# A one-core transformer layer in split fp32: six changes around the starts and boundaries of its stages

## The reference

```
h = x
h = h + 0.5 * rmsnorm(swiglu(rmsnorm(h, g_ffn1_pre), gate1, up1, down1), g_ffn1_post)   # width 5632
z = rmsnorm(h, g_mix_pre) @ w_qkv + b_qkv                                              # 4352 columns
oa = dilated_attention(qa, ka, va)      # 16 heads, three patterns merged by their log-sums
ob = sliding_window_gqa(qb, kb, vb, sinks)   # 16 query heads, 2 key heads
o  = concat(rmsnorm(oa, g_out_a), rmsnorm(ob, g_out_b)) @ w_o + b_o
h  = h + rmsnorm(o, g_mix_post)
h  = h + 0.5 * rmsnorm(swiglu(rmsnorm(h, g_ffn2_pre), gate2, up2, down2), g_ffn2_post)
h  = h + rmsnorm(sigmoid(rmsnorm(h, g_ple_pre) @ w_ple_gate) * (p @ w_ple_proj), g_ple_post)
rmsnorm(x, g) = x * rsqrt(mean(x*x) + 1e-6) * g
```

## Time and profile before

| | us |
|---|---|
| median of 3 runs | 1939.09 (1938.91 to 1940.13) |
| the profiled execution: time | 1938.77 |
| the profiled execution: span | 1937.0 |
| PE busy | 1917.0 (99%) |
| DVE busy | 1052.5 (54%) |
| ACT busy | 876.3 (45%) |
| POOL busy | 9.9 (1%) |

### The profile page before, as it was taken

The page is one execution under the profiler, slowest core; times in us unless marked ns, Lnnn a source line. Parts: engine busy times, 40 slices in busy tenths (PEclk is TensorE's granted clock), DMA queues, the critical chain, the costliest instruction groups (busy, mean ns, idle before and its releaser), DMA issues.

```text
span 1937.0 us, 24879 instructions
## 1 busy us (share of the span) xinstructions
PE 1917.0 (99%) x8929; PEld 1589.9 (82%) x8929; DVE 1052.5 (54%) x1227; ACT 876.3 (45%) x1125; POOL 9.9 (1%) x24
## 2 busy tenths in 40 slices
PE   9999999999999999999999999999999999999998
PEld 7888888888888887888888788888888888888886
DVE  5545445444544446766776754545454454444575
ACT  6444444444444345545454544444444443444563
POOL 0000000000000000000000000000000000000000
PEclk9999999999999999999999999999999999999999
DMA  7666666666566654655555566666666665656554
GB/s 241 187 191 188 191 188 187 189 188 191 194 198 197 204 193 142 186 162 154 157 185 168 158 193 186 187 192 189 190 188 191 188 193 197 199 195 205 189 193 142
DMA packets 188483, 361.05 MB, mean 186 GB/s; under 512 B 11440, under 2 KB 16000, under 8 KB 188032
## 3 DMA queue, kind: packets, MB, share of 16 engines
q1 hardware_dynamic: 187408, 356.69, 60.4%
q10 hardware_dynamic: 1008, 3.46, 0.5%
HBM read 358.01 MB, written 2.10 MB: 186 GB/s over the span
## 4 chain that ended last, share of the span: by engine, by line
PE 96%; DVE 1%; DMA 1%; ACT 1%; issue 1%; POOL 0%; ACTq 0%; DVEq 0%; POOLq 0%; SPq 0%
PE bank L451 30%; PE bank L453 30%; PE bank L452 30%; PE bank L550 2%; PE bank L725 1%; PE bank L735 1%; DMA raw<-in_w_qkv 1%; DVE w_rest L1168 0%; PE bank L750 0%; PE bank L749 0%; ACT w_high L865 0%; PE bank L509 0%; PE bank L587 0%; PE bank L748 0%; PE bank L519 0%
## 5 line engine op out<-in xcount | busy, mean ns | idle before, releaser
L1168 DVE TENSOR_TENSOR w_rest<-raw,w_high 128x1024 fp32r<-128x1024 f32 x656 | 802.3, 1225 | 756.5 <-ACT w_high L865 755.4
L865 ACT CAST w_high<-raw 128x1024 fp32r<-128x1024 f32 x656 | 686.9, 1049 | 908.8 <-PE bank L453 900.4
L451 PE MATMUL bank<-w_high,x_high 128*128 128x512 f32 (+1 forms) x1920 | 754.9, 393 | 2.1 <-DVE w_rest L1168 1.8
L453 PE MATMUL bank<-w_high,x_rest 128*128 128x512 f32 (+1 forms) x1920 | 745.6, 388 | 0.0
L452 PE MATMUL bank<-w_rest,x_high 128*128 128x512 f32 (+1 forms) x1920 | 744.3, 388 | 0.0
L451 PEld LDWEIGHTS bank<-w_high,x_high 128*128 128x128 f32 x1920 | 360.8, 188 | 75.9 <-issue 4.6
L453 PEld LDWEIGHTS bank<-w_high,x_rest 128*128 128x128 f32 x1920 | 360.7, 188 | 75.0
L452 PEld LDWEIGHTS bank<-w_rest,x_high 128*128 128x128 f32 x1920 | 361.1, 188 | 70.4
L451 PE MATMUL bank<-w_high,h_high 128*128 128x512 f32 x704 | 274.2, 390 | 0.0
L453 PE MATMUL bank<-w_high,h_rest 128*128 128x512 f32 x704 | 273.9, 389 | 0.0
L452 PE MATMUL bank<-w_rest,h_high 128*128 128x512 f32 x704 | 273.9, 389 | 0.0
(11 more groups left out here) (147 smaller groups left out, 638.0 us busy)
## 6 DMA issues: line engine op xcount, KB each, us to landing
raw<-in_w_ffn_gate SPq DMA_DIRECT2D x176, 512.0 KB, 4.4
raw<-in_w_ffn_up SPq DMA_DIRECT2D x176, 512.0 KB, 3.7
raw<-in_w_ffn_down SPq DMA_DIRECT2D x176, 512.0 KB, 4.3
raw<-in_w_qkv SPq DMA_DIRECT2D x68, 512.0 KB, 3.8
raw<-in_w_o SPq DMA_DIRECT2D x32, 512.0 KB, 3.7
raw<-in_w_ple_gate SPq DMA_DIRECT2D x32, 512.0 KB, 4.5
resid<-in_x SPq DMA_DIRECT2D x8, 256.0 KB, 7.0
gain_row<-in_g_ffn_post SPq DMA_DIRECT2D x8, 256.0 KB, 4.0
```

What stands on the lines that cost most here:

```text
L451: nc.tensor.matmul(o[:, 0:width], xh, wh, start=first and c == 0, stop=False)
L453: ins = nc.tensor.matmul(o[:, 0:width], xr, wh, start=False, stop=last and c == chunks - 1)
L865: nc.scalar.copy(slot(n, k)[0], raw[:, k]).then_inc(w_high_done, 1)
L1168: nc.vector.tensor_tensor(to_rest, raw[:, k], to_high.bitcast(F32), ALU.subtract).then_inc(w_rest_done, 1)
```

## The change

Six edits:

1. The bias row of the first qkv block, whose DMA waits until PE has used all slots before `S_QKV`, is issued by SP behind all 8 loads of the block, and no longer between the fourth and the fifth.
2. `sum_up` is gone from DVE. ACT's squares carry the scale (1/width, times 4 where the branch is halved), and POOL adds the parts one after another (`factor`), each addition waiting for the one before, then takes the power. Where a factor covers both tiles, POOL now works them out one after the other.
3. At both boundaries, the fourth early slot (s=3) is cast and subtracted inside the boundary and no longer ahead of it. DVE does it behind the residual of tile 1.
4. The six small DMAs of FFN1's start are issued one behind each of six later casts.
5. In a lead block that starts at slot 0 (FFN1 and the last gate product), x units are turned in pairs: 2 and 3 behind slot 0, 4 and 5 behind slot 2, 6 and 7 behind slot 4.
6. The first attention-output unit of the second half is turned one slot earlier (`O_TURN_AT`: offset 2 where it was 3).

```diff
-    O_TURN_AT = [NSLOT - KS + 1 + k for k in range(HU)] + [NSLOT + d for d in (3, 4, 7, 12)]
+    O_TURN_AT = [NSLOT - KS + 1 + k for k in range(HU)] + [NSLOT + d for d in (2, 4, 7, 12)]
...
-                load_block(n, w_qkv, RING, col, width=width)
+                before = RING if i else KS
+                load_block(n, w_qkv, before, col, width=width)
                 if i == 0:
                     sp.wait_ge(w_used, S_QKV)
                 sp.dma_start(bias_row[:, col:col + width], b_qkv[:, col:col + width].to_broadcast([P, width])
                              ).then_inc(bias_landed[i % 2], 16)
-                load_block(n, w_qkv, slots, col, s0=RING, width=width)
+                load_block(n, w_qkv, slots, col, s0=before, width=width)
...
+            def factor(job, t):
+
+                n, eps = squares[job] // T, share(job) * EPS
+                part = [stat[:, job, t, b:b + 1] for b in range(n)]
+                pool.wait_ge(squared, Q[job] + T * (n - 2) + t + 1)
+                step(nc.gpsimd.tensor_scalar(msq[:, job, t:t + 1], part[0], eps, None, ALU.add))
+                for b in range(1, n):
+                    if b == n - 1:
+                        pool.wait_ge(squared, Q[job] + T * b + t + 1)
+                    step(nc.gpsimd.tensor_tensor(msq[:, job, t:t + 1], msq[:, job, t:t + 1], part[b], ALU.add))
+                return nc.gpsimd.tensor_tensor(rstd[:, job, t:t + 1], msq[:, job, t:t + 1], minus_half[:, t:t + 1],
+                                               ALU.pow)
...
-                    if s + 2 < KS and s + 2 >= turned_before:
+                    if s0:
+                        if s + 2 < KS:
+                            turn_k(s + 2)
+                    elif s % 2 == 0 and s + 3 < KS:
                         turn_k(s + 2)
+                        turn_k(s + 3)
...
-                high(n0 + RING, 0)
+                high(n0 + RING - 1, RING - 1)
                 x_lead(u0, 0, 1, f, gain)
                 x_lead(u0, 1, 1, f, gain)
+                high(n0 + RING, 0)
                 x_lead(u0, 2, 1, f, gain)
...
-                ahead(n0, KS - 1, KS + 1)
+                for m in range(KS + 1):
+                    ahead(n0, KS - 1 + m, 1)
+                    if between and m < 6:
+                        between(m)
...
-                    ahead(n, S_TURN_P + 1, (FS - 3 if f else FS - 1) - S_TURN_P, k0)
+                    ahead(n, S_TURN_P + 1, (FS - 3 if f else FS - 2) - S_TURN_P, k0)
...
-                sum_up(job, 0, 1)
                 dve.wait_ge(branch_ready, CREDIT + blocks - 1)
                 dve.wait_ge(rstd_ready, factors_up_to(job, 0))
                 for k in range(LEAD):
...
+                rest(n0 + RING - 1, RING - 1)
+                x_rest_lead(u0, 0, 1, f, gain)
                 update(job, LEAD, 0)
-                x_rest_lead(u0, 0, 1, f, gain)
+                x_rest_lead(u0, 1, 1, f, gain)
                 rest(n0 + RING, 0)
-                x_rest_lead(u0, 1, 1, f, gain)
+                x_rest_lead(u0, 2, 1, f, gain)
                 update(job, LEAD + 1, 0)
-                x_rest_lead(u0, 2, 1, f, gain)
                 rest(n0 + RING + 1, 1)
```

More of the change, by code:

```diff
@@ L423, in factors @@
                     done[0] += 1
-                    pool.wait_ge(summed, done[0])
-                    nc.gpsimd.tensor_tensor(rstd[:, job, t0:t1], msq[:, job, t0:t1], minus_half[:, t0:t1], ALU.pow
-                                            ).then_inc(rstd_ready, 1)
-            factors(factors_up_to(J_MIX))
+                    for t in range(t0, t1):
+                        ins = factor(job, t)
+                    ins.then_inc(rstd_ready, 1)
+            factors(factors_up_to(J_POST1))
             pool.wait_ge(w_used, S_QKV)
@@ L1561, in _ @@
                         ins.then_inc(branch_ready, 1)
[L1562 removed]
+                if L < L_END - 1:
+                    rest(S_QKV + L + RING, L % RING)
                 if L == L_KEYS:
```

61 lines of the change are left out of this document (22 added, 39 removed).

## The result

The changed kernel takes 1927.42 us (median of 4 runs, 1927.20 to 1927.57) where the kernel before took 1939.00 (4 runs, 1936.84 to 1940.13): a ratio of 0.9943, 95% interval 0.9931 to 0.9955. The forecast was 1928.3, within 1925.5 to 1931.8. The profiled execution took 1927.20, with a span of 1925.3: 11.7 us less than the span before.

A forecast was written before the change was run, and what follows sets the result against it. PE, busy 99%, bounds the kernel, so only its stops and slow stretches can give time. Terms -2.7 - 6.1 - 1.7 - 0.8 + 0.2 + 0.3 = -10.8 us from 1938.77 gave 1928.0, 1928.3 on the median; range 1925.5 to 1931.8.

The forecast's parts named there:

- FFN1's start: Edits 4 and 5 bring slot 8 from 36.06 to 33.3: -2.7 us, between -1.4 and -3.0.
- POOL's loss of 0.3: Additions on POOL delay its power by 0.1 us: +0.2 entered for both boundaries, +0.1 for the end.
- The DMAs' part: At FFN1's start, casts put ahead of the six small DMAs remove slot 8's 1.5 us delay.
- The pairs' part: At FFN1's start, turning one slot earlier brings unit 7 up to 1.44 us earlier; slots run at 2.7 to 2.83.
- First boundary: Edits 1 to 3: 1.4 us gained before tile 1 is done, 4.7 from there to the fourth slot; together -6.1.
- E: Time when PE has done tile 1 at a boundary and the third unit is turned; 744.96 at the first, before.
- Second boundary: Moving the fourth early rest lets the fourth slot start at 1101.0 against 1102.72: -1.7 us, bounds -0.2 and -2.9.
- the chain of 9.4 us: DVE's work at each boundary from tile 1's residual to the fourth slot's x_rest: updates, x_rests and three rests, 9.4 us.
- The clock held: Rival: the clock falls at the new boundary waits of 1.6 us; one fall gives 1929.8, two 1931.5; chance 0.2.
- half of the terms: Rival: DVE's boundary chain is longer, paired turns stall, half the gain behind tile 1 is lost: 1933; chance 0.07.
- No stall moved on: Rival: PE meets each hindrance one slot later, time within 0.2% of before, 1936 or more; chance 0.03.
- Additions of a microsecond: Sign of being wrong: POOL additions that long, where under 0.54 us was forecast; slow-additions rival, gain gone at 2.6, chance 0.03.

The follow-up runs named there:

- early cast back: Changed kernel with edit 3 undone at both boundaries, so the fourth early slot is cast and subtracted ahead of them: 1931.70 us, ratio 0.9965.
- bias alone: Kernel before with edit 1 alone, the bias DMA behind all eight loads of the first qkv block: 1932.99 us, ratio 0.9969.
- early slot alone: Kernel before with edit 3 alone (fourth early cast and rest moved into the boundary), plus POOL's index patterns moved there: 1931.40 us, ratio 0.9964.
- both back: Changed kernel with edits 1 and 3 both undone: 1936.02 us, ratio 0.9989.
- bias back: Changed kernel with edit 1 undone, the bias DMA again between the fourth and fifth qkv load: 1928.56 us, ratio 0.9949.
- slow sum: Changed kernel with three more dependent additions of a zero on POOL behind the last square of every factor: 1931.39 us, ratio 0.9963.

## Why the prediction was right, point by point

The total came out 0.9 us from the forecast, closer than its parts: FFN1's start gave 0.7 us less than its term, the boundaries 0.5 and 0.8 more, and POOL's loss of 0.3 did not come. That these nearly cancel is luck. The chains that the terms rest on were the right ones, the sharing out among the edits was not.

**What bounds.** Right: four places held all of the gain, PE's standing still there and the clock that fell behind two of the stops, and the table shows the rest of the program unchanged.

**FFN1's start: -2.7 forecast, -2.0 measured.** The DMAs' part is as worked out. The pairs' part was mis-sized: I let all eight slots run at 2.7 to 2.83 us. Timeline of the changed kernel:

```profile
27.25 1.23 DVE L1201 TENSOR_TENSOR w_rest<-raw,w_high 128x1024 fp32r<-128x1024 f32 x1
28.62 0.47 PE L470 MATMUL bank<-w_high,x_high 128*128 128x512 f32 x1
30.17 2.96 ACT L888 CAST w_high<-raw 128x1024 fp32r<-128x1024 f32 x3
31.24 3.50 DVE L1201 TENSOR_TENSOR w_rest<-raw,w_high 128x1024 fp32r<-128x1024 f32 x3 [0.85 <-ACT w_high L888]
31.46 0.39 PE L470 MATMUL bank<-w_high,x_high 128*128 128x512 f32 x1
31.46 3.33 POOL L435 TENSOR_TENSOR msq<-msq,stat 128x1 f32<-128x1 f32 x3
34.18 0.39 PE L470 MATMUL bank<-w_high,x_high 128*128 128x512 f32 x1
```

Slots 6, 7 and 8 start at 28.62, 31.46 and 34.18, in step at last. But slot 7 is only 0.38 us nearer to slot 0 than in the earlier trace rows: slots 2, 4 and 6 still begin when their rests are ready (the rest from 27.25 ends at 28.48, slot 6 starts at 28.62), 0.2 us late each, so an x unit that is ready earlier has nothing to shorten there. The measured term lies within its bounds, but the two edits do not add: either alone gives 1.5.

**First boundary: -6.1 forecast, -6.6 measured.** Ahead of E 1.4 forecast; E stands 3.24 us behind the stretch's start where it stood 4.78, so 1.5. But edit 3, to which the term was booked, is sure of only 0.3 to 0.6 of it. In the two profiles that lack edit 3 but have edit 1, E stands at 3.80 (early cast back) and 3.87 (bias alone), against 3.24 and 3.56 with edit 3 (changed kernel, early slot alone), with a wait of 0.2 to 0.3 us where the kernel before had 1.2. What differs is the landing of the fourth early slot: its cast starts 2.0 us ahead of the stretch there and 1.1 ahead in the kernel before and in both back. The DMAs of the last two down weights, in the 20.5 us that end at the stretch's start (count, KB each, median us from issue to landing), in the kernel before and then with edit 1 alone:

```profile
raw<-in_w_ffn_down SPq DMA_DIRECT2D x2, 512.0 KB, 4.6
```

```profile
raw<-in_w_ffn_down SPq DMA_DIRECT2D x2, 512.0 KB, 3.7
```

These two loads stand ahead of everything that edit 1 touches, so this is scatter between executions and not the edit. Without edit 3 the boundary pays up to 0.9 us of it. With edit 3 it pays nothing: E stands at 3.24 both in the changed kernel, where the four early qkv loads took 4.5 us, and with the bias back, where they took 3.5; this pair also has the late landing with edit 1 and the early one without it. (A late landing may also be part of what the unprofiled runs with the early cast back lost; no trace shows it.) Behind E, 16.2 to 11.5 forecast, 16.2 to 11.1 measured, with a wait of 0.9 and not 1.6 us. The chain I named is the one that ends last. Its size was 0.3 too large, though DVE also stood idle 0.32 us in it for ACT's cast; the reason shows better at the second boundary. What the prediction got wrong in kind is the attribution: it gave all that lies behind E to edit 1. Edit 3 alone does most of it (5.4 us, edit 1 alone 6.8), and given edit 1, edit 3 made this boundary 0.3 longer in the profile, with a load that landed early.

**Second boundary: -1.7 forecast, -2.5 measured** (-2.8 by four other profiles of the same code, 20.8 in the table). Up to an estimated 1.7 us of it is the clock, which the term did not count apart. E was forecast 4.9 us behind the stretch's start (1088.6 less 1083.7) and came 4.9 behind it. Behind E the slot was forecast at +12.4 and came at +11.6. Timeline of the changed kernel:

```profile
1079.29 0.38 PE L506 MATMUL bank<-ident,resid 128*128 128x128 f32 x2
1082.11 1.28 DVE L1225 SCALAR_TENSOR_TENSOR resid<-branch,rstd,resid 128x256 f32<-128x256 f32 x3 [0.74 <-POOL rstd L436]
1086.33 1.23 DVE L1201 TENSOR_TENSOR w_rest<-raw,w_high 128x1024 fp32r<-128x1024 f32 x1
1087.48 0.60 DVE L1238 SCALAR_TENSOR_TENSOR x_rest<-bank,gain_T,x_high 128x128 fp32r<-128x128 f32 x2
1088.00 0.87 DVE L1225 SCALAR_TENSOR_TENSOR resid<-branch,rstd,resid 128x256 f32<-128x256 f32 x2
1088.79 1.22 DVE L1201 TENSOR_TENSOR w_rest<-raw,w_high 128x1024 fp32r<-128x1024 f32 x1
1089.92 0.87 DVE L1216 SCALAR_TENSOR_TENSOR x_rest<-bank,gain_T,x_high 128x256 fp32r<-128x256 f32 x2
1090.85 0.50 PE L470 MATMUL bank<-early_high,x_high 128*128 128x512 f32 x1 [0.68 <-DVE x_rest L1216]
```

The step that was mis-sized is the chain of 9.4 us: it added durations. A rest of 1.23 us at 1086.33 is followed at 1087.48, 1.15 later; an x_rest pair of 0.60 is followed 0.52 later, a residual pair of 0.87 at 0.79, a rest of 1.22 at 1.13. Back to back, each group gives back 0.08 us, since the next instruction starts before the end of the one before. From 1082.11 the slot is 8.7 us off.

**POOL: +0.3 forecast, nothing or a small gain measured.** Where PE waits for the factor, the addition takes 0.19 us (0.27 taken) and the hand-over to the power 0.07 (0.24 taken, from the program's start). The rule of the Trainium skill that I weighed there (GPSIMD Engine Reference, section 3.1, "use DVE for elementwise") does not decide at one column: by the rows of the last tile the two ways differ by 0.03 us. I also had wrong where a slower chain is exposed, as the dearer addition showed: behind E at the first boundary it is mostly covered, ahead of E there is no cover of 0.5 us, and the end counts twice.

**Attention's end: -0.8 forecast, -0.75 measured. Gate product: +0.2 forecast, +0.2 measured,** as one wait of 0.5 us for the residual of the pair's second unit, part of it made good.

**The rivals.** The clock held at both waits of 0.9 and 0.7 us. What a fall costs was read about rightly: the second boundary is 23.7 and 24.0 with a fall (before, bias alone) and 22.2 and 22.3 without (both back, early cast back), 1.3 to 1.7 us apart, where 1.7 was used. Whether it falls is not settled by the wait alone: at a wait of 2.0 us ahead of the turns it fell with edit 1 alone and held with edit 3 undone. Two sums of the rivals are off: one and two falls on 1928.3 are 1930.0 and 1931.6, and half of the terms of 4.7 and 1.7 us at the boundaries would give 1931.5 before any stall of the turns, not 1933. No stall moved on: the stretches between are unchanged.

**The signs.** One of the signs of being wrong came true. Additions of a microsecond were to speak against the forecast, and three at FFN1's start took 1.1 us each (last section). They cost nothing, because they stand where PE needs no factor; the prediction's price for them holds only at the exposed places, where each took 0.19. Slot 8 started at 34.18 and not near 33.3, and the waits ahead of the fourth slots were 0.9 and 0.7 us and not 1 to 2.

## What to carry to other kernels

Two remedies can take away the same wait, one by bringing the late thing forward, one by giving the waiting engine other work ahead of it. Then leaving either out shows it as nearly worthless there, and only leaving out both, or adding one to the kernel before, shows what each can do. In a chain of back-to-back instructions count from start to start, not durations. And what stands directly ahead of the instruction that PE waits for is worth a look: here a rest that was needed one slot later stood in front of one needed now, and turning the two round was worth 1.55 us.

## What the hardware showed that I had not expected

POOL's small operations stretch while DVE runs a rest, the subtraction of two 128x1024 operands in SBUF. In the timeline of FFN1's start above, three additions from 31.46 take 3.33 us together, beside the three rests that DVE runs from 31.24 for 3.50, where such an addition takes 0.19 with DVE idle (the row at 1915.83 of the slow sum). The Trainium skill (GPSIMD Engine Reference, Specifications) says that GpSimd's SBUF interfaces are shared with VectorE, with contention where VectorE's instruction has two SBUF inputs; the trace agrees: each of the three additions takes 1.1 us instead of 0.19 and ends 0.05 us behind the end of one of the three rests. Here it cost little. The factor of FFN1 was late by it, and ACT's first output waited for it (the timeline goes on):

```profile
34.86 0.57 POOL L436 TENSOR_TENSOR rstd<-msq,minus_half 128x1 f32<-128x1 f32 x1
35.47 0.69 ACT L962 ACTIVATE branch<-bank,rstd 128x512 f32<-128x512 f32 x1 [2.33 <-POOL rstd L436]
```

But PE needed that output for nothing yet: from slot 8 to the first boundary there are 704.0 us, and 704.1 in the kernel before. The factors that PE waits for are worked out while DVE runs no rest, and the additions ahead of their powers took 0.19 us.
